# A hybrid decoder block in fp32: the wait before w_o's B12, and where S4 of the attention output is summed

## The reference

```python
h = rmsnorm(x, attn_norm_g)
u_b, u_c, u_x, q, k, v, g_conv, g_attn = split(h @ w_in)
y_conv = (u_b * short_conv(u_c * u_x, conv_w)) @ w_conv_out
y_attn = sliding_window_attention(q, k, v, sinks, rel_bias) @ w_attn_out
mixed = sigmoid(g_conv) * y_conv + sigmoid(g_attn) * y_attn
x = x + mixed @ w_o
x = x + square(relu(rmsnorm(x, mlp_norm_g) @ w_up)) @ w_down
return rmsnorm(x, final_norm_g)
```

## Time and profile before

| | |
|---|---|
| median of 3 runs | 757.71 us (757.3 to 758.04) |
| profiled execution | 757.86 us, span 756.1 us |
| TensorE busy | 745.3 us (99%) |
| VectorE busy | 646.3 us (85%) |
| ScalarE busy | 419.8 us (56%) |
| mean granted TensorE clock | 0.997 |
| bytes moved by DMA | 131.22 MB, mean 174 GB/s |

### The profile page before, as it was taken

The page is one execution under the profiler, slowest core; times in us unless marked ns, Lnnn a source line. Parts: engine busy times, 40 slices in busy tenths (PEclk is TensorE's granted clock), DMA queues, the critical chain, the costliest instruction groups (busy, mean ns, idle before and its releaser), DMA issues.

```text
span 756.1 us, 10473 instructions
## 1 busy us (share of the span) xinstructions
PE 745.3 (99%) x4067; PEld 646.6 (86%) x4067; DVE 646.3 (85%) x748; ACT 419.8 (56%) x535; POOL 81.9 (11%) x117
## 2 busy tenths in 40 slices
PE   8999999999999999999999999999999999999996
PEld 7888888888888888888878899889988999899985
DVE  5766688889899686989899999998799879986997
ACT  7424555453644656664548776654465355545555
POOL 3202000121112101001000101010101010000102
PEclk9999999999999999999999999999999999999998
DMA  7727513143237996766965746767677767676703
GB/s 256 248 83 279 168 55 112 57 108 114 72 123 223 293 263 169 222 166 187 301 180 138 222 142 168 211 178 193 190 175 190 200 168 207 183 198 191 196 1 112
DMA packets 69408, 131.22 MB, mean 174 GB/s; under 512 B 2604, under 2 KB 22132, under 8 KB 69364
## 3 DMA queue, kind: packets, MB, share of 16 engines
q1 hardware_dynamic: 50400, 84.18, 33.4%
q0 software_dynamic: 18752, 46.15, 27.6%
q10 hardware_dynamic: 212, 0.28, 0.1%
HBM read 124.29 MB, written 6.32 MB: 173 GB/s over the span
## 4 chain that ended last, share of the span: by engine, by line
PE 90%; DVE 4%; DMA 3%; issue 2%; ACT 1%; SPq 0%; DVEq 0%; ACTq 0%
PE pair L959 38%; PE pair L918 21%; PE pair L727 8%; PE pair L729 8%; PE pair L728 8%; DMA home_raw<-in_w_attn_out 2%; PE pair L774 2%; DVE home_lo L1756 1%; PE pair L749 1%; PE pair L748 1%; PE pair L758 1%; DMA xn<-in_x 1%; PE pair L820 1%; DVE mixed L1948 0%; DVE s_lo_tile L1812 0%
## 5 line engine op out<-in xcount | busy, mean ns | idle before, releaser
L1191 ACT ACTIVATE high<-home_raw 128x2048 fp32r<-128x2048 f32 x91 | 174.3, 1915 | 147.3 <-PE pair L959 96.7
L1756 DVE TENSOR_TENSOR home_lo<-home_raw,high 128x2048 fp32r<-128x2048 f32 x91 | 208.4, 2290 | 37.2 <-ACT high L1191 36.8
L959 PE MATMUL pair<-high,s_hi_tile 128*128 128x512 f32 x440 | 110.3, 391 | 0.0
L959 PE MATMUL pair<-high,s_lo_tile 128*128 128x512 f32 x440 | 110.0, 390 | 0.1
L959 PE MATMUL pair<-home_lo,s_hi_tile 128*128 128x512 f32 x440 | 109.3, 389 | 0.0
L727 PE MATMUL pair<-h,wgt 128*128 128x512 f32 x256 | 101.5, 397 | 0.0
L729 PE MATMUL pair<-h,wgt 128*128 128x512 f32 x256 | 99.9, 390 | 0.0
L728 PE MATMUL pair<-h,wgt 128*128 128x512 f32 x256 | 99.8, 390 | 0.0
L959 PEld LDWEIGHTS pair<-high,s_lo_tile 128*128 128x128 f32 x440 | 82.4, 188 | 17.6 <-DVE s_lo_tile L1812 0.5
L959 PEld LDWEIGHTS pair<-home_lo,s_hi_tile 128*128 128x128 f32 x440 | 82.5, 188 | 17.1
L959 PEld LDWEIGHTS pair<-high,s_hi_tile 128*128 128x128 f32 x440 | 81.8, 188 | 17.2 <-ACT pair L1283 0.5
(11 more groups left out here) (215 smaller groups left out, 1001.8 us busy)
## 6 DMA issues: line engine op xcount, KB each, us to landing
raw<-in_w_in SPq DMA_DIRECT2D x34, 512.0 KB, 4.6
home_raw<-in_w_up SPq DMA_DIRECT2D x16, 1024.0 KB, 5.5
home_raw<-in_w_down SPq DMA_DIRECT2D x16, 1024.0 KB, 5.1
home_raw<-in_w_up POOLq DMA_DIRECT2D x12, 1024.0 KB, 8.3
home_raw<-in_w_down POOLq DMA_DIRECT2D x12, 1024.0 KB, 8.3
home_raw<-in_w_in POOLq DMA_DIRECT2D x7, 1024.0 KB, 8.3
home_raw<-in_w_in SPq DMA_DIRECT2D x7, 1024.0 KB, 6.5
home_raw<-in_w_conv_out SPq DMA_DIRECT2D x4, 1024.0 KB, 5.1
```

The source lines that it names most:

```text
L959: last = mm(pair[region(s, i)][:, b, :], a_[:, k, b * P:(b + 1) * P], w[:, k, :], start=(fresh and kind == 0 and k == 0), stop=(kind == 2 ...
L1191: a(high[n % 2][:, :], home_raw[home_of(s, name)][:, :], ACT.Copy).then_inc(m_hi, 1)
L1756: v.tensor_tensor(home_lo[home][:, :], home_raw[home][:, :], f32(high[n % 2][:, :]), ALU.subtract).then_inc(m_lo, 1)
```

## The change

Two edits in the order of work. SP's wait ahead of WO's B12 asks for both parts of AO's T1 (`t1_in`) in place of the first alone (`t1_base`); and on VectorE the sum S4 of AO comes ahead of `low_part(AO, M6)`.

```diff
             load_blocks(CO)
             load_blocks(AO)
-            sp.wait_ge(t1_base, 16 * (AO + 1))
+            sp.wait_ge(t1_in, 16 * (AO + 1))
             load_block(WO, 0, 1)
             wait_used(sp, AO, M6)
...
             gate_conv(2)
+            s4(AO)
             low_part(AO, M6)
-            s4(AO)
             gate_attn(0)
```

## The result

The changed kernel takes 763.54 us (median of 4 runs, 762.6 to 764.4) against 757.66 us: a ratio of 1.0077, 95% interval 1.006 to 1.0095. It is slower by 5.9 us, where 2.5 us were forecast, and above the forecast range of 757.0 to 762.8. In the profiled executions the span grew from 756.1 to 762.7 us.

The account below looks back on a forecast made before the run. TensorE was taken as the bound, with 90% of the chain, waiting 1.6 us for VectorE's last merge. VectorE's 1.0 us lead was lost to a late T3: +2.5 us on the median 757.71 gives 760.2 us, range 757.0 to 762.8.

Parts of the forecast that it names:

- Part 1: AO's T1 without B12 beside it: lands 8.3 us after issue, at 360.5 instead of 363.65, 3.2 us earlier.
- part 2: S4 moved into VectorE's 1.08 us idle before low_part(AO, M6): worth 0.2 us by itself, in front of a wait.
- the lead: VectorE earlier by 2.6 us at low_part(AO, M5), 1.1 at low_part(AO, M7), 1.0 at sum_t2(WO), the most the change can bring.
- part 3: WO's B12 held back delays POOL's T3, which meets B11 and B21; sum_t2(WO) starts 2.5 us later, at 379.3.
- I take 13.4: T3 lands at 379.1: WO's T3, issued at 365.7, takes 13.4 us like GA's T3; sum_t2(WO) then starts at 379.3.
- rival 4: T1's first part and residual share too, or plain loads go first: T3 lands 381 to 384, +4.5 to +7 us; chance 0.13.
- The sum of transfers: T3's 5.1 us plus 2.7 each for B11 and B21: 10.5 us from 367.6, last landed at about 378.5.
- The sum's last steps: VectorE 2.5 us late at sum_t2(WO); TensorE waits some 2 us at N4, rest at transposes; last merge ends at 399.1.
- 2 (T3 first, B21 late): T3 goes through first, B21 lands 378.5 to 380.7, sum_t4 decides: -0.7 to +1.5 us, say 758.2 us; chance 0.22.
- 3 (hidden transfers): T3 down by 375.6 and B21 by 378, lead of 1.0 us comes through: 756.7 us; chance 0.11.
- What is won at 396.6 is won at the end: After the last merge at 396.6 the chain is TensorE's to 741.8 us, so gains or losses there reach the end.

Follow-up runs that it names:

- the run with a sliver of T3: Changed kernel, with POOL adding only 32 of the 512 columns of T3's second part for WO, output not the layer's: 757.06 us, ratio 0.9993.
- the sums moved: Changed kernel, with sum_t2(WO) moved ahead of low_part(WO, M1) and sum_t4(WO) ahead of low_part(WO, N2): 758.45 us, ratio 1.0008.

## Why the prediction was right or wrong

**Part 1 and part 2 held.** T1 landed 8.6 us after its issue (8.3 forecast; in six more traces with no other load beside it 8.3 to 8.8, which shows how far single traces scatter); the lead was 2.6 us at `low_part(AO, M5)` and 1.1 us at `low_part(AO, M7)`, as worked out. The move of S4 is worth nothing measurable by itself (757.81 us). That the lead is worth at most 1.0 us agrees with the 0.8 us in the trace of the run with a sliver of T3; its median, 757.06 us, is not clear of noise.

**The mechanism of part 3 held in the main, its one chosen number did not.** B12's landing, forecast at 365.4, came at 366.2 (5.4 us, and it began at 360.76 and not 360.5), so T3 was issued at 366.44 instead of 365.7. That is 0.7 us. The step that failed is "I take 13.4: T3 lands at 379.1": T3 took 16.8 us and landed at 383.2. The 0.7 and the 3.4 make the 4.1 us between the forecast start of `sum_t2(WO)`, 379.3, and the measured 383.35.

The runs show what the 16.8 us consist of. Taking the neighbours away one after the other gave 15.3 us (T1's first part: 1.5), 14.0 (residual: 1.3) and 11.7 (B21: 2.3); from there to the 8.3 us of a load without company it is 3.4 us, which is then B11's. These are differences of single traces. With all four neighbours T3 took 16.8, 16.5 (the wait alone) and 16.1 us (the sums moved), so the 1.5 could be as little as 0.8; the sum of all, 7 to 8 us above a load alone, stands clear of that.

GA's T3, from which 13.4 was taken, was not the same case. It met two plain loads of 1 MB, issued at 251.59 and 256.95, and the tail of smaller ones; POOL's first part of GA's T1 was issued 8.6 us behind it, at 262.67, and here 1.4 us behind, at 367.85. The run here with two plain loads beside T3 gave 14.0 us: for that company the row was right to 0.6 us. The prediction names T1's first part and the residual as takers, gives 383.9 as the latest landing with both, and then puts at the centre 379.1, close to its 378.5 without them: the first half of rival 4, both sharing too, with a chance of 0.13, is what happened. It had said that T1's part would come at about 368 to 370, and that the residual goes out at 371.56. Both were sure to meet T3, and the row chosen should have been one in which they do.

The prediction also had T3 issued 0.4 us ahead of B11, and shared between them. It was issued 0.3 us behind, and in the run with B11 alone beside it T3's bytes moved after B11's.

The sum of transfers was a little short too. Three loads were to take 10.5 us from 367.6 on, and the last to land at 378.5 with no other company. In the run where just these three were in flight bytes still moved after 378 (92 GB/s in 378:380), and T3 landed at 380.4, though it was issued only 0.7 us later than forecast. (The 4.9 us in that paragraph, called a row of B12's, is that of the load alone at 316.91; the figures worked out from it stay the same.)

**The sum's last steps held.** A delay at `sum_t2(WO)` passes on in full: from there to the end of the last `merge` VectorE took 19.83 us in both kernels (376.77 to 396.60, and 383.35 to 403.18). 6.58 us at `sum_t2` are 6.59 at the transposes and 6.6 in the span. The 5.9 us of the medians are less, since these two profiled executions lie at 757.86 and 764.40 us. The four times of the changed kernel are 762.60, 762.72, 764.36 and 764.40; the trace, and its 16.8 us, belong to the upper pair. TensorE's wait at N4 for `sum_c22` was forecast as 2 us and is 5.9.

**Rivals.** 2 (T3 first, B21 late) is refuted: B21 landed at 378.6, 4.6 us ahead of T3. 3 (hidden transfers) is refuted for this order of VectorE, and shown to be a matter of that order: with the sum 9.6 us later (385.43 against 375.8) a T3 of 16.1 us costs nothing. The estimate of 4.4 us for 1 MB from GpSimd, from the Trainium skill's page "DMA: Bandwidth & Descriptors", section "Anatomy of one DMA", doesn't fit accumulating loads here: they took 8.3 us alone and 16.8 us in company.

**"What is won at 396.6 is won at the end" was too broad.** It held for delays, and for the 0.8 us by which all of VectorE's work came earlier. It didn't for a lead made by moving VectorE's work behind the last `merge`: with `sum_t4` moved the transposes came 2.1 us earlier, and TensorE waited 1.55 us a few microseconds on. In that run VectorE has no idle time from 394.7 to 418.4 us, and most of what is won in one place is paid with a wait in the next.

## What to carry to other kernels

Before a load is held back to give another one the engines, look at what it is itself awaited by, and which transfers it will then meet: here 3 us for T1 cost 14 us for T3, which before had ended just as the other loads began. For a load in company, take a row with the same number of neighbours, issued at the same distance, or add up all the bytes that will be in flight. And whether a late load costs anything is decided by where its first reader stands in the order of its engine; look at that order before the one on the queue.

## What the runs showed of the hardware

An accumulating load of 1 MB, one trace each: 8.3 to 8.8 us alone (AO's T1 in seven traces), 11.7 with one plain load issued 0.35 us ahead of it, 14.0 with two, 15.3 with three, 16.1 to 16.8 with these and a plain load behind it on its own queue. The plain load issued just ahead kept its 5.0 to 5.5 us.

TensorE's granted clock fell in its wait and stayed down after it, as the windows of the changed kernel show (busy PE first, PEclk before the last two values):

```profile
384.00:388.00 4.00, 0.00 (x0) 0.00 (x0) 3.87 (x3) 1.38 (x1) 1.27 (x1) 0.95 0.89 315
388.00:390.00 2.00, 0.75 (x2) 0.65 (x3) 1.97 (x3) 0.00 (x0) 0.00 (x0) 0.50 0.92 332
390.00:394.00 4.00, 4.00 (x14) 3.22 (x13) 3.96 (x4) 0.00 (x0) 0.00 (x0) 0.50 1.06 217
394.00:396.00 2.00, 2.00 (x11) 1.73 (x10) 2.00 (x2) 1.29 (x2) 0.00 (x0) 0.90 1.13 208
```

0.50 is the lower of its two levels, 1.2 GHz. The first pass of 8 matmuls after the wait spans 3.78 us where 1.98 is usual. That cost nothing here, since VectorE's 19.83 us set the end of the stretch and left TensorE that time: its waits at the transposes fell from 1.6 to 0.4 us. After a wait of 1.2 us, in the kernel before, the clock stayed at 1.00; after one of 3.1 us, in the run with the residual held, its mean over 387:394 was 0.76.
